# Nine places for split weight chunks, a six-chunk tail per block and a boundary without splits in a float32 two-block transformer

## The chip, the cores and the metric

The kernel runs on one core of a Trainium2 chip. The metric is the time of one execution on the device in microseconds, as the median of several runs. Engines are named as in the profile: PE (TensorE), PEld (its weight loads), DVE (VectorE), ACT (ScalarE), POOL (GpSimd) and SP (SyncE, whose queue issues all DMAs here).

## The reference

Two transformer blocks over 256 tokens of width 1024, batch 1, everything in float32. The norms, the residuals and the feed-forward parts bear on this change:

```python
# first block
x = x + gt1 * _rmsnorm(mix_x, g_post_mix)            # mix_x = concat(pool mixer, attention) @ w_out
y = _sq_relu_mlp(_modulate(x, g_pre_mlp, sh2, sc2), w_mlp_in, w_mlp_out)   # square(relu(h @ w1)) @ w2, width 4096
x = x + gt2 * _rmsnorm(y, g_post_mlp)
# second block
x = x + 0.5 * swiglu(rmsnorm(x, ffn1_norm), ...)     # width 2816
proj = rmsnorm(x, mix_norm) @ w_in
x = x + concat(attention_a, attention_b) @ w_out
x = x + 0.5 * swiglu(rmsnorm(x, ffn2_norm), ...)
x = rmsnorm(x, final_norm)
```

`_modulate(x, g, sh, sc)` is the root-mean-square norm of x times g (1 + sc), plus sh.

## The kernel before

**Chunks and splits.** All weights stream from HBM in the order of `stream_plan` as chunks of 128 x 1024 float32 (512 KB) through seven raw buffers. Float32 accuracy comes from three fast products: ACT rounds a chunk to `hi` (L449), DVE writes the rest `raw - hi` to `lo` (L866), and PE multiplies hi by Th, hi by Tl and lo by Th, where Th and Tl are the activations split in the same way. A split chunk lives in one of `RING = 5` places; ACT may write chunk h only when PE has used chunk h-5 (semaphore `s_used`). `AHEAD = 4` says how far ahead of PE's chunk the splits are put into the programs of ACT and DVE. SP loads a raw buffer again when DVE has written the `lo` of the chunk that was in it.

**Every engine has its own program**, written out by hand in the order in which it runs; waits are on counting semaphores. No scheduler reorders anything.

**Blocks and boundaries.** Four times a product into x is followed by norms and the next product: boundary 0 (w_out, then the MLP), 1 (MLP, then ffn1), 2 (ffn1, then the second mixer's input product), 3 (w_out2, then ffn2). The 256 tokens are two halves i of 128. The last product of a block sums into four PSUM banks, two per half. Its last `TAIL = 4` chunks are the tail: `tail_first`/`out_first` does the four chunks for half 0 and signals `s_part`, then `tail_second`/`second_out` does the same chunks for half 1. Below, "part" is the moment of that signal. In the boundary, for each half: ACT squares the PSUM sums (`gated_squares`, L461), DVE multiplies them by a gain (`gated`, L1086), POOL takes the root (L399), DVE adds to x (`added`, L1103), ACT squares x, DVE sums (L1075), POOL takes the root again, DVE and ACT scale half of x each (`normed`, L1110 and L626). Boundaries 2 and 3 have no first norm: DVE adds PSUM to x at once (L1093). Then PE transposes eight tiles of 128 x 128 (`turned`, L1641) into four banks by turns, so that the fifth waits until the first has been read. ACT writes Th (L634 in boundary 0, where a shift is added, else L637), DVE writes Tl (L1131). In boundary 0 DVE first computes the shifted value itself (L1126) and then subtracts Th (L1117), tile by tile. PE then multiplies the half by the first four chunks of the next block (h0 to h0+3, 24 matmuls of 512 columns; 416 in boundary 2). The second half goes the same way.

The order of ACT and DVE in a boundary (L640 and L1137), where h0 is the next block's first chunk:

```python
split(h0)
e.wait_ge(s_part, b + 1)
gated(b, 0)
added(b, 0)
split(h0 + 1)
normed(b, 0)
e.wait_ge(s_used, h0)
gated(b, 1)
turned(b, 0)
split(h0 + 2)
added(b, 1)
split(h0 + 3)
normed(b, 1)
split(h0 + 4)
turned(b, 1)
```

**The second attention** (L585, L1032, L1577) runs over 32 tiles (16 heads by two halves) in software-pipelined steps n. In each, PE scores a tile and transposes an earlier one, DVE and ACT do the softmax. `fill2(n)` puts other work into chosen steps: PE's whole products with w_out2 chunks 0 to 3 at n = 17, 19, 21, 25, the first-half products of chunks 4, 5, 6 at n = 28, 29, 33, and one split at n = 17, 19, 21, 25 and 28.

**SP's queue** waits at H[26], which is h0+2 of boundary 0, for `s_G` 4 (a gain row that DVE finishes, L978), issues a row load into `gp`, and only then the chunk (L356 to L358, L373).

`big` is a work buffer of 11,776 float32 per partition. It holds q, k, v and other tiles of the two attentions and of the norms around them, and is idle (but for columns 0 to 2047) from the first attention's end to the second mixer.

## Time and profile before

| | us |
|---|---|
| median of 3 runs (lowest, highest) | 928.18 (926.5, 929.54) |
| the profiled execution's own time | 929.46 |
| its span in the profile | 927.5 |
| PE busy | 863.7 |
| DVE busy | 521.0 |
| ACT busy | 444.2 |
| POOL busy | 44.6 |

The time before is the median; the rows come from the profiled execution, which took 929.46 us and of which the profile spans 927.5. Busy time of PE includes the modelled end of pipelined matmuls, so the idle time between its instructions is read from the timeline, which gives it in brackets with the instruction that ended it.

### The profile page before, as it was taken

How to read it: one execution, taken by the hardware profiler on the slowest of the kernel's cores; microseconds unless marked ns; L12 is line 12 of the kernel's file. 1: busy time of each engine (PE TensorE's matmuls, PEld its weight loads, DVE VectorE, ACT ScalarE, POOL GpSimd, SP SyncE). 2: the span in 40 equal slices, each digit the busy share in tenths (PEclk: the TensorE clock that was granted, in tenths of full speed). 3: DMA queues.
4: the chain of work that ended last, by engine and by line, in shares of the span. 5: the costliest groups of instructions: out<-in, count | busy, mean ns of one | idle time of the engine just before them, and what ended most of it. 6: DMA issues, size and time to landing. Idle time of an engine off the chain costs nothing.

```text
span 927.5 us, 13973 instructions
## 1 busy us (share of the span) xinstructions
PE 863.7 (93%) x5434; PEld 734.9 (79%) x5434; DVE 521.0 (56%) x904; ACT 444.2 (48%) x797; POOL 44.6 (5%) x55
## 2 busy tenths in 40 slices
PE   5898899979999999899999999898798899999996
PEld 3696655749999998679999999785465699999995
DVE  2344167476776565665555554677445565555554
ACT  3553045265545444554444444765445554444442
POOL 1000000000000000000000000055100000000000
PEclk9999799979999999999999999998779999999998
DMA  8966338425787565356555554564012265555521
GB/s 325 397 250 248 116 136 319 159 90 163 262 280 226 182 186 172 102 173 231 182 184 182 196 185 146 207 215 158 0 46 69 92 207 179 194 191 181 185 92 46
DMA packets 45105, 165.87 MB, mean 179 GB/s; under 512 B 4976, under 2 KB 5104, under 8 KB 44784
## 3 DMA queue, kind: packets, MB, share of 16 engines
q1 hardware_dynamic: 45040, 164.98, 51.7%
q8 instruction: 44, 0.72, 0.3%
q14 instruction: 21, 0.17, 0.1%
HBM read 163.91 MB, written 1.05 MB: 178 GB/s over the span
## 4 chain that ended last, share of the span: by engine, by line
PE 83%; DVE 5%; ACT 4%; issue 4%; DMA 2%; POOL 1%; SPq 0%; ACTq 0%; DVEq 0%; POOLq 0%
PE ps L1361 13%; PE ps L1363 13%; PE ps L1362 12%; PE ps L1381 12%; PE ps L1383 12%; PE ps L1385 12%; DMA raw<-in_w_mod_p 2%; PE ps L1608 2%; PE ps L1407 1%; ACT hi L449 1%; DVE lo L866 1%; ACT PT L461 1%; PE ps L1795 1%; PE ps L1801 1%; PE ps L1592 1%
## 5 line engine op out<-in xcount | busy, mean ns | idle before, releaser
L866 DVE TENSOR_TENSOR lo<-raw,hi 128x1024 fp32r<-128x1024 f32 (+1 forms) x247 | 298.9, 1218 | 180.2 <-ACT hi L449 180.0
L449 ACT ACTIVATE hi<-raw 128x1024 fp32r<-128x1024 f32 (+1 forms) x247 | 257.1, 1049 | 78.3 <-PE ps L1385 59.9
L1361 PE MATMUL ps<-Th,hi 128*128 128x256 f32 (+1 forms) x960 | 276.1, 288 | 3.1 <-DVE lo L866 1.7
L1363 PE MATMUL ps<-Th,lo 128*128 128x256 f32 (+1 forms) x960 | 275.0, 287 | 0.0
L1362 PE MATMUL ps<-Tl,hi 128*128 128x256 f32 (+1 forms) x960 | 275.0, 287 | 0.0
L1381 PE MATMUL ps<-hi,Th 128*128 128x512 f32 (+2 forms) x524 | 180.6, 404 | 13.9 <-issue 7.0
L1361 PEld LDWEIGHTS ps<-Th,hi 128*128 128x128 f32 x960 | 184.0, 192 | 8.5 <-issue 3.0
L1362 PEld LDWEIGHTS ps<-Tl,hi 128*128 128x128 f32 x960 | 183.9, 192 | 3.7
L1363 PEld LDWEIGHTS ps<-Th,lo 128*128 128x128 f32 x960 | 183.8, 191 | 1.3
L1383 PE MATMUL ps<-lo,Th 128*128 128x512 f32 (+2 forms) x524 | 175.7, 394 | 0.0
L1385 PE MATMUL ps<-hi,Tl 128*128 128x512 f32 (+2 forms) x524 | 175.4, 394 | 0.0
L1381 PEld LDWEIGHTS ps<-hi,Th 128*128 128x128 f32 x524 | 96.0, 193 | 32.7 <-issue 16.4
L1385 PEld LDWEIGHTS ps<-hi,Tl 128*128 128x128 f32 x524 | 100.2, 191 | 21.1
L1383 PEld LDWEIGHTS ps<-lo,Th 128*128 128x128 f32 x524 | 100.4, 192 | 20.5
L679 ACT ACTIVATE Th<-PT 128x256 fp32r<-128x256 f32 x68 | 28.4, 418 | 98.7 <-DVE PT L1211 81.8
L1172 DVE TENSOR_TENSOR Tl<-PT,Th 128x256 fp32r<-128x256 f32 x68 | 29.0, 426 | 32.9 <-ACT Th L679 32.9
L719 ACT ACTIVATE PT<-ps 128x256 f32<-128x256 f32 x40 | 15.4, 385 | 62.9 <-PE ps L1363 62.9
L1407 PE MATMUL ps<-raw,big 128*32 128x256 f32 x320 | 26.4, 447 | 15.0 <-DMA raw<-in_w_mod_p 14.4
L399 POOL TENSOR_TENSOR st<-st 128x1 f32<-128x1 f32 x12 | 6.6, 551 | 583.3 <-DVE st L1075 583.3
L1407 PEld LDWEIGHTS ps<-raw,big 128*32 128x32 f32 x320 | 8.7, 118 | 30.5 <-issue 16.2
L693 ACT ACTIVATE PT<-ps 128x256 f32<-128x256 f32 x28 | 10.7, 383 | 44.5 <-PE ps L1363 44.5
L461 ACT ACTIVATE PT<-x 128x512 f32<-128x512 f32 x24 | 15.0, 629 | 26.4 <-DVE x L1093 10.4
(189 smaller groups left out, 622.4 us busy)
## 6 DMA issues: line engine op xcount, KB each, us to landing
raw<-in_ffn_down SPq DMA_DIRECT2D x44, 512.0 KB, 3.6
raw<-in_w_mod_p SPq DMA_DIRECT2D x40, 512.0 KB, 6.1
raw<-in_ffn_gate SPq DMA_DIRECT2D x40, 512.0 KB, 3.2
raw<-in_ffn_up SPq DMA_DIRECT2D x40, 512.0 KB, 3.2
raw<-in_w_mlp_out SPq DMA_DIRECT2D x32, 512.0 KB, 4.5
raw<-in_w_mlp_in SPq DMA_DIRECT2D x28, 512.0 KB, 4.4
raw<-in_w_out SPq DMA_DIRECT2D x16, 512.0 KB, 5.6
raw<-in_w_in_q SPq DMA_DIRECT2D x8, 512.0 KB, 5.7
```

What stands on the lines that cost most here:

```text
L449: e.activation(hi[h % RING][:, 0:w], raw[n % RAW][:, 0:w], ACT.Copy).then_inc(s_hi, 1)
L461: e.activation(junk[len(squared) % 2][:, 0:512], src, ACT.Square, scale=scale, accum_out=out).then_inc(s, 1)
L679: e.activation(Th[:, f % 8, L:], fbuf[f % 4], ACT.Copy).then_inc(s_ha, 1)
L866: e.tensor_tensor(lo[h % RING][:, 0:w], raw[n % RAW][:, 0:w], hi[h % RING][:, 0:w], ALU.subtract).then_inc(s_lo, 1)
L1172: e.tensor_tensor(Tl[:, f % 8, L:], fbuf[f % 4], Th[:, f % 8, L:], ALU.subtract).then_inc(s_hl, 1)
L1361: e.matmul(o, a, Th[:, k, c0:c1], start=(k == 0), stop=False)
L1362: e.matmul(o, a, Tl[:, k, c0:c1], start=False, stop=False)
L1363: return e.matmul(o, b, Th[:, k, c0:c1], start=False, stop=(k == KT - 1))
L1381: e.matmul(ps[banks[j][n]][:, 0:n_w], lh, a[:, at[n]:at[n] + n_w], start=f, stop=False)
L1383: e.matmul(ps[banks[j][n]][:, 0:n_w], lh, b[:, at[n]:at[n] + n_w], start=False, stop=False)
L1385: m = e.matmul(ps[banks[j][n]][:, 0:n_w], ll, a[:, at[n]:at[n] + n_w], start=False, stop=z)
L1407: m = e.matmul(ps[bank][32 * j:32 * j + 32, c0:c0 + L], w, raw[at % RAW][:, j * L:(j + 1) * L], start=(kh == 0), stop=(kh == 1))
```

## The change

1. **Places.** Eight more pairs of split places are laid over `big`: four are free from w_out chunk 5 to the end of ffn1's block (`EXT1` to `END1`), four others from w_out2 chunk 5 on (`EXT2`). With the ring's five that makes nine. Between `END1` and `EXT2` the ring has five as before. `SLOT[h]` is the place that was written longest ago, `PREV[h]` the chunk that was in it, and `lead(h)` the last chunk that may be split while PE works at h: h+8 with nine places, h+4 with five. All `+ AHEAD` become `lead(...)`, and the splits beside a down product are at most two at a time.
2. **Tail.** `TAIL` goes from 4 to 6, in w_out and w_out2 too, where chunks 2 and 3 are now done for half 0 only before part. The second halves of the first five tail chunks come next, then four transposes, then the sixth, then the other four transposes.
3. **Boundary.** Chunks h0, h0+1 and h0+2 are split before the wait for part, h0+3 after `normed` of half 0, h0+4 at the end. Four tiles are turned before the second half's `gated`, four behind it.
4. **Boundary 0's turn.** ACT writes the shifted even tiles and DVE the odd ones to a small buffer; ACT then copies two tiles at once to Th, and DVE subtracts two at once.

The diff, cut to its core:

```diff
-TAIL = 4
+TAIL = 6
...
+        blocks = [(3072 + 2048 * i, 4096 + 2048 * i) for i in range(4)] + [(8192, 9216), (0, 1024), (2048, 10240),
+                                                                         (3072, 4096)]
+        HI = [u[:, :] for u in hi] + [in_big(f"hi{i + 5}", a)[:, :] for i, (a, _) in enumerate(blocks)]
+        LO = [u[:, :] for u in lo] + [in_big(f"lo{i + 5}", a)[:, :] for i, (_, a) in enumerate(blocks)]
+        SLOT, PREV, newest = [], [], [-1] * len(HI)
+        for h in range(NH):
+            free = list(range(RING)) + list(range(5, 9) if EXT1 <= h < END1 else range(9, 13) if EXT2 <= h else [])
+            slot = min(free, key=lambda n: (newest[n], n))
+            SLOT.append(slot)
+            PREV.append(newest[slot])
+            newest[slot] = h
+
+        def lead(h):
+
+            n = h
+            while n + 1 < NH and PREV[n + 1] < h:
+                n += 1
+            return n
...
-                    if h >= RING:
-                        e.wait_ge(s_used, h - RING + 1)
-                    e.activation(hi[h % RING][:, 0:w], raw[n % RAW][:, 0:w], ACT.Copy).then_inc(s_hi, 1)
+                    if PREV[h] >= 0:
+                        e.wait_ge(s_used, PREV[h] + 1)
+                    if h == EXT2:
+                        e.wait_ge(s_thP, 8)
...
+                    if h == EXT2 + 3:
+                        e.wait_ge(s_pv, 16)
+                    e.activation(HI[SLOT[h]][:, 0:w], raw[n % RAW][:, 0:w], ACT.Copy).then_inc(s_hi, 1)
...
-            def turned(b, i):
+            def turned(b, i, k0, k1):
...
+                    elif k % 2 == 0:
+                        e.wait_ge(s_tp, t_n(b, i, k))
+                        if 8 * i + k >= 4:
+                            e.wait_ge(s_tTl, 8 * i + k - 2)
+                        e.activation(moved(k), src, ACT.Identity, bias=sh2[:, k:k + 1],
+                                     scale=gain[:, k:k + 1]).then_inc(s_tfa, 1)
                     else:
...
+                        e.wait_ge(s_tfa, 4 * i + k // 2 + 1)
+                        e.wait_ge(s_tfd, 4 * i + k // 2 + 1)
+                        e.activation(Th[:, k - 1:k + 1, here], moved_pair(k), ACT.Copy).then_inc(s_tTh, 2)
             def boundary(b):
                 h0 = LASTCH[b] + 1
-                split(h0)
+                split(h0 + 2)
                 e.wait_ge(s_part, b + 1)
                 gated_squares(b, 0)
                 scale_squares(b, 0)
-                split(h0 + 1)
                 normed(b, 0)
+                split(h0 + 3)
+                if b == 0:
+                    e.wait_ge(s_A2, 1)
+                turned(b, 0, 0, 4)
                 e.wait_ge(s_used, h0)
                 gated_squares(b, 1)
-                if b == 0:
-                    e.wait_ge(s_A2, 1)
-                turned(b, 0)
-                split(h0 + 2)
+                turned(b, 0, 4, KT)
                 scale_squares(b, 1)
-                split(h0 + 3)
                 normed(b, 1)
+                turned(b, 1, 0, KT)
                 split(h0 + 4)
-                turned(b, 1)
                 return h0 + 4
...
                 elif what == "down" and f < FM - TAIL:
-                    split(CH["w_mlp_out", f] + AHEAD)
+                    split_by(2, lead(CH["w_mlp_out", f]))
...
-                for at, k in ((17, 0), (19, 1), (21, 2), (25, 3), (28, 4)):
+                for at, k in ((17, 4), (19, 5), (21, 6), (25, 7)):
                     if n == at:
-                        split(CH["w_out2", k] + AHEAD)
+                        split(CH["w_out2", k])
...
-                for k in (1, 2, 3):
-                    out_whole("w_out", k)
+                out_whole("w_out", 1)
+                for k in (2, 3):
+                    out_first("w_out", k)
...
                 first().then_inc(s_part, 1)
-                second()
-                turned(b, 0)
+                second(0)
+                turned(b, 0, 0, 4)
+                second(1)
+                turned(b, 0, 4, KT)
...
-                for at, k in ((17, 0), (19, 1), (21, 2), (25, 3)):
+                for at, k in ((17, 0), (19, 1)):
...
-                for at, k in ((28, 4), (29, 5), (33, 6)):
+                for at, k in ((21, 2), (25, 3), (28, 4), (29, 5), (33, 6)):
```

**How the order moves.** On PE in boundary 0, around the transposes (rows with x2 are the two banks of a tail chunk's second half, rows without are the first product of the MLP). Before:

```order
L1381 MATMUL ps<-hi,Th 128x512 x2
L1383 MATMUL ps<-lo,Th 128x512 x2
L1385 MATMUL ps<-hi,Tl 128x512 x2
L1641 MATMUL ps<-cols,arena 128x128 x8
L1381 MATMUL ps<-hi,Th 128x512
```

With the change (`hi_51` and `lo_59` are places in `big`):

```order
L1423 MATMUL ps<-lo_58,Th 128x512 x2
L1425 MATMUL ps<-hi_50,Tl 128x512 x2
L1682 MATMUL ps<-cols,arena 128x128 x4
L1421 MATMUL ps<-hi_51,Th 128x512 x2
L1423 MATMUL ps<-lo_59,Th 128x512 x2
L1425 MATMUL ps<-hi_51,Tl 128x512 x2
L1682 MATMUL ps<-cols,arena 128x128 x4
L1421 MATMUL ps<-hi_52,Th 128x512
```

One tail chunk's second half now stands between the two groups of four transposes.

On DVE in boundary 0, from the last splits before part to the second `added`. Before:

```order
L866 TENSOR_TENSOR lo<-raw,hi 128x1024 x4
L1086 TENSOR_TENSOR sc<-ps,G 128x512 x2
L1075 TENSOR_SCALAR st<-st 128x1
L1103 SCALAR_TENSOR_TENSOR x<-sc,st,x 128x512 x2
L1075 TENSOR_SCALAR st<-st 128x1
L866 TENSOR_TENSOR lo<-raw,hi 128x1024
L1110 TENSOR_SCALAR arena<-x,st 128x512
L1086 TENSOR_TENSOR sc<-ps,G 128x512 x2
L1075 TENSOR_SCALAR st<-st 128x1
L1126 TENSOR_SCALAR sc<-ps,st 128x128 x2
L1117 TENSOR_TENSOR Tl<-sc,Th 128x128
```

With the change:

```order
L912 TENSOR_TENSOR lo<-raw,hi 128x1024 x2
L1132 TENSOR_TENSOR sc<-ps,G 128x512 x2
L1121 TENSOR_SCALAR st<-st 128x1
L1149 SCALAR_TENSOR_TENSOR x<-sc,st,x 128x512 x2
L1121 TENSOR_SCALAR st<-st 128x1
L1156 TENSOR_SCALAR arena<-x,st 128x512
L912 TENSOR_TENSOR lo<-raw,hi 128x1024
L1170 TENSOR_SCALAR sc<-ps,st 128x128 x2
L1175 TENSOR_TENSOR Tl<-sc,Th 128x2x128 x2
L1132 TENSOR_TENSOR sc<-ps,G 128x512 x2
```

The split has moved from before the scaling (`arena<-x,st`) to behind it, six splits instead of four precede the first gain product (four of them name places in `big` and stand above this piece), and half a turn comes before the second gain product.

On ACT at boundary 3, from the attention's last Th to the scaling. Before:

```order
L602 ACTIVATE Th<-ps 128x256
L461 ACTIVATE PT,st<-x 128x512 x2
L449 ACTIVATE hi<-raw 128x1024
L626 ACTIVATE arena<-x,st 128x512
L637 ACTIVATE Th<-ps,cols 128x128 x8
```

With the change:

```order
L643 ACTIVATE Th<-ps 128x256
L490 ACTIVATE hi_56<-raw 128x1024
L490 ACTIVATE hi<-raw 128x1024 x2
L502 ACTIVATE PT,st<-x 128x512 x2
L667 ACTIVATE arena<-x,st 128x512
```

Three splits now stand between the attention's end and the boundary's first squares; one stood before the scaling.

## Rows read from the trace of the kernel before

**Rows 1.** The page: busy time, share and instructions of each engine.
```profile
PE 863.7 (93%) x5434; PEld 734.9 (79%) x5434; DVE 521.0 (56%) x904; ACT 444.2 (48%) x797; POOL 44.6 (5%) x55
```

**Rows 2.** Windows: stretch, us, busy us PE PEld DVE ACT POOL, clock, DMA share, GB/s.
```profile
181.89:212.39 30.50, 24.00 (x88) 17.58 (x88) 20.91 (x51) 17.42 (x39) 2.20 (x4) 0.83 0.23 77
379.56:405.99 26.43, 21.14 (x88) 16.15 (x88) 16.80 (x35) 15.39 (x39) 2.20 (x4) 0.94 0.29 100
576.57:597.04 20.47, 17.76 (x88) 14.99 (x88) 14.34 (x34) 12.95 (x31) 1.10 (x2) 1.00 0.46 152
721.74:743.90 22.16, 19.65 (x89) 14.98 (x87) 13.46 (x29) 12.59 (x31) 1.11 (x2) 1.00 0.29 96
...
179.17:181.89 2.72, 2.72 (x13) 2.25 (x13) 0.00 (x0) 0.00 (x0) 0.00 (x0) 1.00 1.02 416
```

**Rows 3.** Timeline of PE, boundaries 0 and 1: start us, us, what, [idle before].
```profile
189.07 0.66 PE L1641 MATMUL ps<-cols,arena 128*128 128x128 f32 x4 [1.76 <-DVE arena L1110]
...
191.35 1.74 PE L1641 MATMUL ps<-cols,arena 128*128 128x128 f32 x4 [1.62 <-DVE sc L1126]
...
200.61 0.47 PE L1381 MATMUL ps<-hi,Th 128*128 128x512 f32 x1 [2.50 <-DVE lo L866]
...
386.74 0.66 PE L1641 MATMUL ps<-cols,arena 128*128 128x128 f32 x4 [1.76 <-DVE arena L1110]
...
388.79 1.16 PE L1641 MATMUL ps<-cols,arena 128*128 128x128 f32 x4 [1.40 <-DVE Tl L1131]
...
398.46 0.60 PE L1641 MATMUL ps<-cols,arena 128*128 128x128 f32 x4
...
400.45 0.47 PE L1381 MATMUL ps<-hi,Th 128*128 128x512 f32 x1
```

**Rows 4.** Timeline of DVE, boundary 0.
```profile
181.91 1.41 DVE L1086 TENSOR_TENSOR sc<-ps,G 128x512 f32<-128x512 f32 x2 [3.06 <-PE ps L1385]
...
188.53 0.48 DVE L1110 TENSOR_SCALAR arena<-x,st 128x512 f32<-128x512 f32 x1
...
196.10 1.40 DVE L1103 SCALAR_TENSOR_TENSOR x<-sc,st,x 128x512 f32<-128x512 f32 x2
```

**Rows 5.** Timeline of POOL, boundary 0.
```profile
186.74 0.55 POOL L399 TENSOR_TENSOR st<-st 128x1 f32<-128x1 f32 x1 [2.53 <-DVE st L1075]
...
198.59 0.55 POOL L399 TENSOR_TENSOR st<-st 128x1 f32<-128x1 f32 x1 [7.38 <-DVE st L1075]
```

**Rows 6.** Groups in boundary 0: line, op, shapes, xcount | busy us, mean ns | idle.
```profile
L634 ACT ACTIVATE Th<-ps,st 128x128 fp32r<-128x128 f32 x16 | 6.5, 458 | 2.2 <-PE ps L1641 2.0
L1126 DVE TENSOR_SCALAR sc<-ps,st 128x128 f32<-128x128 f32 x16 | 6.3, 403 | 1.4 <-ACT Th L634 1.4
...
L866 DVE TENSOR_TENSOR lo<-raw,hi 128x1024 fp32r<-128x1024 f32 x4 | 4.9, 1223 | 1.5 <-ACT hi L449 1.5
...
L449 ACT ACTIVATE hi<-raw 128x1024 fp32r<-128x1024 f32 x4 | 4.2, 1042 | 0.0
```

**Rows 7.** The page's part 5: a copy of 128x256 from SBUF.
```profile
L679 ACT ACTIVATE Th<-PT 128x256 fp32r<-128x256 f32 x68 | 28.4, 418 | 98.7 <-DVE PT L1211 81.8
```

**Rows 8.** Timeline of ACT, boundary 3.
```profile
719.15 0.38 ACT L602 ACTIVATE Th<-ps 128x256 fp32r<-128x256 f32 x1 [0.95 <-PE ps L1608]
...
724.77 0.72 ACT L626 ACTIVATE arena<-x,st 128x512 f32<-128x512 f32 x1
```

**Rows 9.** Timeline of DVE, boundary 3.
```profile
721.74 1.29 DVE L1093 SCALAR_TENSOR_TENSOR x<-ps,x 128x512 f32<-128x512 f32 x2 [1.75 <-PE ps L1385]
```

**Rows 10.** Timeline of PE in the second attention.
```profile
697.75 0.30 PE L1592 MATMUL ps<-cols,sc 128*128 128x128 f32 x1 [0.62 <-ACT PT L596]
```

**Rows 11.** Timeline of SP's DMA issue of chunks h0+2 and h0+3, boundary 0.
```profile
171.78 1.15 SPq L373 DMA_DIRECT2D raw<-in_w_mlp_in_rows  x2
```

**Rows 12.** Tile raw, 160 to 200 us: time from issue to landing.
```profile
DMA to landing us min/median/max: 3.5/5.7/7.4
```

**Rows 13.** Windows: a long stretch of the last feed-forward block.
```profile
748.00:900.00 152.00, 152.00 (x1074) 143.17 (x1073) 84.18 (x93) 69.35 (x93) 0.00 (x0) 1.00 0.55 187
```

177 lines of the change are left out of this document (91 added, 86 removed).

## The prediction

> **What bounds the kernel now.** The page comes first: PE is busy 863.7 of 927.5 us, DVE 521 and ACT 444 [rows 1]. In a feed-forward stretch PE is busy for all of 152 us at clock 1.00, while DVE needs 84 us and ACT 69 [rows 13]. There nothing is left to win by splitting further ahead. The windows then show where PE does wait: the four boundaries last 30.50, 26.43, 20.47 and 22.16 us from part to the end of the eight products ahead, 99.6 us together [rows 2]. The work in one is known. Two chunks' second halves take 2.72 us, so one takes 1.36 [rows 2]. A boundary holds four of them (5.4), eight products of the same 512 columns at six matmuls a chunk over both halves, which is 24 matmuls or 5.45 a half (4.4 in boundary 2, 416 columns), and 16 transposes, for which I put 2.0. That makes 18.3 us, 16.2 in boundary 2, 71.1 in all. So 28 us are waits and slow clock, and that is the ceiling of the gain.
>
> The timeline of PE names them [rows 3]. In boundary 0 PE waits 1.76 us for the scaled x (L1110), 1.62 for turned tiles, and 2.50 for a `lo` (L866). In boundary 1 it waits 1.76 and 1.40 before the first products. [...]
>
> **Part by part.** I count from part, t = 0, and chunk halves move with it: the two tail chunks that are added put 2.72 us of PE work behind part that stood before it. So a boundary gains what it took before, plus 2.72, minus what it takes now, wherever PE was full before part. It was ahead of boundary 0 (clock 1.00, PE busy 2.72 of 2.72 [rows 2]), and I take the same of 1 and 2.
>
> *The chain of half 0.* In boundary 0 gains start on DVE at 181.91 [rows 4] and POOL's second root ends at 187.29 [rows 5], 5.4 later. DVE scaled x only at 188.53 [rows 4], since a split of 1.22 us [rows 6] stood in between. Now it is scaled at 5.4 + 0.48 = 5.9. PE does five second halves until 6.8, so the wait of 1.76 goes in both boundaries, with 0.9 us to spare. The sixth half (6.8 plus four transposes to 8.7) covers the first turn.
>
> *Boundary 0.* After scaling, ACT splits h0+3 (its scaling 0.72 and the split 1.04 us [rows 6, 8] put the end at 7.2) and DVE follows to 8.4. The turn by pairs has no row. Its upper bound is the old one: a tile cost ACT 0.46 and DVE 0.40 [rows 6], plus the subtraction. Its lower bound is a pair copy alone at 0.42 [rows 7]. I take 0.46 + 0.42 a pair on ACT, and 0.40 + 0.40 + 0.42 on DVE, since each pass is nearest to those rows. Four tiles are then finished at 10.4; PE starts on products at 9.9 and has two chunks until 12.6. DVE's second gains (1.41 [rows 4]) end at 11.8, ACT turns the other tiles until 13.6, DVE until 14.2. PE waits 0.8 and ends half 0 at 16.1. From `added` to the root was 196.10 to 199.14, 3.0 us [rows 4, 5]: 17.3, scaled at 17.7, so PE waits 1.6. From the first transpose to the first product takes 2.0 (398.46 to 400.45 [rows 3]): 19.7, and 5.4 more is 25.1.
> Two things are added. Chunk h0+2 must now be split before part is even waited for. It is issued at 171.78 [rows 11], behind SP's wait for the gain row, and lands a median 5.7 us later [rows 12]. With 1.04 and 1.22 [rows 6] its `lo` is there at 179.8, while part moves to 181.89 - 2.72 = 179.2. That is 0.7 late, and DVE starts its gains that much later. And the waits of 1.6 and about 1.3 around the second transposes look like those of boundary 1, so I take one fall of the clock, 1.4. Boundary 0: 27.2, against 30.5 + 2.7 = 33.2. **Gain 6.0.**
>
> *Boundary 1.* ACT and DVE turn as before, four tiles each time. DVE is finished with the first four at 9.5, PE starts at 9.7 and does all four chunks until 15.15 without a wait. The second gains end at 10.9, the other four tiles at 12.4, x is scaled at 15.9. PE waits 0.8, then 2.0 and 5.4: 23.4. I take no fall of the clock. 26.4 + 2.7 - 23.4: **gain 5.75.**
>
> *Boundary 2* has one root only. Scaled x comes long before 6.8; products run from 9.2 to 13.6, x of half 1 is scaled by 12.9; 2.0 and 4.4 more make 20.0. 20.5 + 2.7 - 20.0: **gain 3.2.**
>
> *Boundary 3.* The attention's last Th ends at 719.53 [rows 8]. Three splits now follow on ACT, and DVE's three end at 719.53 + 1.04 + 3 x 1.22 = 724.2, while it began to add at 721.74 [rows 9]: 2.5 late. From there to the scaling was 3.0 (724.77 [rows 8]), so x is scaled at 6.0, before 6.8; the delay is hidden, by 0.8. Products start at 9.7, end at 15.15, then 2.0 and 5.45: 22.6 against 22.2. The work that moved in comes from the attention, where PE isn't full: behind the product at n = 21 it already waits 0.62 for ACT [rows 10]. What the attention gives back for 2.72 us is between 0 and 2.7; I take 1.1, nearer to nothing because of that wait, with one split less in it. **Gain 0.7.**
>
> *Nothing* is booked for the deeper places in long stretches (PE full there, [rows 13]) and for the last block's six-chunk tail: after the last product the norm of half 1 runs as before. If the splits did not fit beside PE, that cover would be gone (third rival).
>
> The sum is 6.0 + 5.75 + 3.2 + 0.7 = 15.6 us. Against the profiled execution (929.46) it gives 913.8; that one lies 1.3 above the median, and against the median of 928.2 it is **912.6 us**.
>
> **Rivals.** *The clock keeps falling.* Boundary 1 fell after waits of 1.76 and 1.40 with four transposes between [rows 3], and 2 and 3 did not. If it falls in 1 as well (1.4), and in the attention, where three half products of 1.36 would take 4.1 more, with its 1.1 not given back, the gain is 15.6 - 6.6 = 9.0: 919. For it: the attention's PE work gets thinner. Against: the waits get shorter in total. [...]
>
> *All cover works.* No fall of the clock in boundary 0 (1.4 back), chunk h0+2 in time (0.7) and the attention gives back all 2.7 (1.6 more): 19.3, so 909; with half of the second transposes' waits hidden too, 907.
>
> *The debt is paid behind the boundary* (slower). After each boundary ACT and DVE must split four chunks more to be eight ahead, two at each place, ahead of the activations on the same engine that PE waits for. Four `lo` are 4.9 us of DVE [rows 6], four times 19.6 us. If PE waited for all of it, the result would be 4.0 slower, 932; it decides from 15.6 us on. Against it: DVE is idle 68 of 152 us there [rows 13], and the hidden tiles have a lag of two to five steps.
>
> *The change doesn't do what it says*: the second halves wait as the first did. If only the waits of half 0 go (1.76 twice, 1.62, 1.40), the gain is 6.5: 922.
>
> **Chances.** Forecast 0.62, all cover 0.12, clock 0.12, only half 0 0.05, no change 0.05, slower 0.04. A measurement can tell 0.3% (2.8 us) from no change: faster 0.91, same 0.05, slower 0.04. The bounds of the attention (0 to 2.7), of the clock (0 to 5) and of the turn reach from 907 to 919; the range of eight in ten is 905.5 to 919.5, which takes in both nearer rivals.
>
> **What would show it.** PE without a wait of over 0.5 us before the first transposes of all boundaries; part of boundary 0 near 179.2, DVE's gains a little behind; waits of 1.6 and 0.8 before the transposes of half 1 in boundaries 0 and 1; granted clock 0.9 or more in boundary 0 and 1.00 in 1; about 27, 23, 20 and 22.5 us per boundary. A PE wait for `lo` or Tl inside the feed-forward blocks, or a boundary 1 over 26 us, would make the forecast wrong.

## The result and the profile after

The changed kernel takes **912.23 us** (median of 4 runs, 911.67 to 913.14) where the kernel before takes 927.51 beside it (926.5 to 929.54): a ratio of 0.9837, 95% interval 0.9823 to 0.9851. The forecast was 912.6. The profiled execution took 913.14 with a span of 911.2; the one before had 929.46 and 927.5.

The page, part 1, against [rows 1]:

```profile
PE 859.1 (94%) x5434; PEld 732.0 (80%) x5434; DVE 515.2 (57%) x888; ACT 440.3 (48%) x797; POOL 44.5 (5%) x55
```

PE is busy 4.6 us less, though it does the same work, and the span is 16.3 us shorter. The windows of the four boundaries, from part to the end of the products ahead, answer to [rows 2] (stretch, us, busy us of PE, PEld, DVE, ACT and POOL, clock, DMA share, GB/s):

```profile
179.31:206.63 27.32, 23.84 (x100) 18.19 (x100) 16.41 (x34) 15.47 (x37) 2.19 (x4) 0.94 0.33 124
371.00:394.26 23.26, 22.23 (x100) 17.23 (x100) 14.35 (x33) 13.58 (x37) 2.20 (x4) 1.00 0.13 43
561.13:581.37 20.24, 19.63 (x100) 17.28 (x100) 12.39 (x32) 11.27 (x29) 1.10 (x2) 1.00 0.11 33
705.27:727.74 22.47, 21.86 (x101) 17.29 (x100) 13.12 (x30) 11.39 (x30) 1.12 (x2) 1.00 0.36 117
```

With the two halves that moved in (2.72 us for the two), boundary 0 went from 33.2 to 27.3, boundary 1 from 29.2 to 23.3, boundary 2 from 23.2 to 20.2 and boundary 3 from 24.9 to 22.5. PE's timeline of boundary 0, the rows with a wait, against [rows 3] (start, us, what, [idle before <- who ended it]):

```profile
189.14 0.44 PE L1682 MATMUL ps<-cols,arena 128*128 128x128 f32 x2 [0.55 <-ACT sc L680]
...
193.12 0.50 PE L1421 MATMUL ps<-hi,Th 128*128 128x512 f32 x1 [0.75 <-DVE Tl L1175]
...
197.45 0.66 PE L1682 MATMUL ps<-cols,arena 128*128 128x128 f32 x4 [1.31 <-DVE arena L1156]
...
198.42 0.41 PE L1682 MATMUL ps<-cols,arena 128*128 128x128 f32 x2 [0.31 <-ACT sc L680]
...
199.27 0.33 PE L1682 MATMUL ps<-cols,arena 128*128 128x128 f32 x1 [0.44 <-ACT sc L680]
```

There is no wait before the first transposes any more (1.76 before), none of 2.50 for a `lo`, and one of 1.31 for the scaled x of half 1. Boundary 1 had 1.76 and 1.40 [rows 3], 1.52 for a `lo` and 0.61; boundary 2 had 1.29 before its fifth transpose, 0.18 and 0.63 for a `lo`, and 0.61. From the kernel before:

```profile
397.00 0.47 PE L1381 MATMUL ps<-hi,Th 128*128 128x512 f32 x1 [1.52 <-DVE lo L866]
...
583.74 1.02 PE L1641 MATMUL ps<-cols,arena 128*128 128x128 f32 x4 [1.29 <-DVE Tl L1131]
...
587.21 0.43 PE L1381 MATMUL ps<-hi,Th 128*128 128x416 f32 x1 [0.18 <-DVE lo L866]
...
589.22 0.42 PE L1381 MATMUL ps<-hi,Th 128*128 128x416 f32 x1 [0.63 <-DVE lo L866]
```

Of these, boundary 2 keeps the 0.61, and boundary 1 has two left:

```profile
386.67 0.66 PE L1682 MATMUL ps<-cols,arena 128*128 128x128 f32 x4 [0.41 <-DVE arena L1156]
...
387.94 0.49 PE L1682 MATMUL ps<-cols,arena 128*128 128x128 f32 x2 [0.61 <-DVE Tl L1164]
```

The start of boundary 0 on ACT and DVE. The split of chunk h0+2 comes ahead of part, and waits for its transfer:

```profile
177.33 1.06 ACT L490 ACTIVATE hi<-raw 128x1024 fp32r<-128x1024 f32 x1 [4.22 <-DMA raw<-in_w_mlp_in_rows]
...
178.42 1.23 DVE L912 TENSOR_TENSOR lo<-raw,hi 128x1024 fp32r<-128x1024 f32 x1 [1.32 <-ACT hi L490]
...
179.56 0.69 DVE L1132 TENSOR_TENSOR sc<-ps,G 128x512 f32<-128x512 f32 x1
```

Part is at 179.31 and gains start at 179.56. In the attention, the two chunks at n = 21 and 25 are now multiplied for half 0 only. PE waits longer there, 1.26 us each time where it was 0.62 [rows 10]:

```profile
681.83 0.30 PE L1633 MATMUL ps<-cols,sc 128*128 128x128 f32 x1 [1.26 <-ACT PT L637]
...
688.81 0.30 PE L1633 MATMUL ps<-cols,sc 128*128 128x128 f32 x1 [1.26 <-DVE PT L1089]
```

For the account, the program is cut at the ends of the boundaries. With the stretch that leads to it, boundary 0 gained 5.8 us, boundary 1 6.0, boundary 2 3.9, and boundary 3 with the attention 0.5; the last stretch gained 0.1. That makes the 16.3.

### The profile page after: what moved, and what is told of

Same layout as the page of the kernel before. It is cut to its first block, busy times and chain, and to the rows that moved or that the text cites. A ratio compares the mean times of both kernels' runs of the same rounds, so it can differ in the third digit from the quotient of the medians.

```text
span 911.2 us, 13975 instructions
## 1 busy us (share of the span) xinstructions
PE 859.1 (94%) x5434; PEld 732.0 (80%) x5434; DVE 515.2 (57%) x888; ACT 440.3 (48%) x797; POOL 44.5 (5%) x55
## 4 chain that ended last, share of the span: by engine, by line
PE 72%; DVE 2%; POOL 1%; ACT 1%; issue 1%; DVEq 0%; ACTq 0%; POOLq 0%
PE ps L1401 11%; PE ps L1402 11%; PE ps L1403 11%; PE ps L1421 11%; PE ps L1423 11%; PE ps L1425 11%; PE ps L1649 2%; PE ps L1839 1%; PE ps L1633 1%; PE ps L1845 1%; PE ps L1682 1%; PE ps L1841 1%; POOL st L456 0%; ACT PT L502 0%; POOL st L462 0%
## 5 line engine op out<-in xcount | busy, mean ns | idle before, releaser
L490 ACT ACTIVATE hi<-raw 128x1024 fp32r<-128x1024 f32 (+1 forms) x247 | 253.8, 1047 | 65.0 <-PE ps L1425 41.5
L1401 PE MATMUL ps<-Th,hi 128*128 128x256 f32 (+1 forms) x960 | 276.2, 288 | 3.1 <-DVE lo L912 1.7
L1401 PEld LDWEIGHTS ps<-Th,hi 128*128 128x128 f32 x960 | 183.8, 191 | 8.6 <-issue 3.0
L1421 PE MATMUL ps<-hi,Th 128*128 128x512 f32 (+2 forms) x524 | 179.9, 402 | 9.5 <-issue 7.3
L1403 PEld LDWEIGHTS ps<-Th,lo 128*128 128x128 f32 x960 | 183.5, 191 | 1.3
L1421 PEld LDWEIGHTS ps<-hi,Th 128*128 128x128 f32 x524 | 94.9, 191 | 27.1 <-issue 9.1
L765 ACT ACTIVATE PT<-ps 128x256 f32<-128x256 f32 x40 | 15.3, 383 | 55.4 <-PE ps L1403 55.4
L647 ACT ACTIVATE sc<-sc,st 128x128 f32<-128x128 f32 (+1 forms) x32 | 14.5, 455 | 27.0 <-DVE st L1106 26.8
```

Source lines behind the costliest of these rows:

```text
L490: e.activation(HI[SLOT[h]][:, 0:w], raw[n % RAW][:, 0:w], ACT.Copy).then_inc(s_hi, 1)
L1401: e.matmul(o, a, Th[:, k, c0:c1], start=(k == 0), stop=False)
L1403: return e.matmul(o, b, Th[:, k, c0:c1], start=False, stop=(k == KT - 1))
L1421: e.matmul(ps[banks[j][n]][:, 0:n_w], lh, a[:, at[n]:at[n] + n_w], start=f, stop=False)
```

## The experiments

Twelve kernels, all made from the changed one. In the table, each profile is one execution, and **two stretches that no experiment touches vary by themselves**. The opening up to part of boundary 0 took 176.9 to 181.1 us in the kernels that have six halves there, with a granted clock of 0.94 to 0.97; in the two with four it took 185.0 and 179.5. The stretch from the end of boundary 2 to the end of boundary 3, the attention in it, took 143.9 to 149.6. And boundary 0 came mostly with a clock of 0.94 or 1.00. So a part is judged by its own boundary at equal clock, and the medians only by their intervals. Boundaries 0, 1 and 2 run from part to the end of their products; the fifth column is the stretch with the attention and boundary 3. Boundary 1 had a clock of 0.94 in the kernel before and 1.00 in all others; boundary 2 had 1.00 in all.

| kernel | b0 us (clock) | b1 | b2 | attention + b3 | median us | ratio to before (95%) |
|---|---|---|---|---|---|---|
| before | 30.50 (0.83) | 26.43 | 20.47 | 146.86 | 927.5 | 1 |
| changed | 27.32 (0.94) | 23.26 | 20.24 | 146.37 | 912.23 | 0.984 (0.982 to 0.985) |
| tail4 | 25.47 (1.00) | 22.00 | 17.41 | 147.56 | 917.43 | 0.988 (0.983 to 0.992) |
| chain_splits | 30.42 (0.89) | 26.85 | 21.94 | 145.53 | 921.29 | 0.994 (0.991 to 0.997) |
| places_only | 31.56 (0.84) | 22.01 | 17.40 | 143.91 | 918.58 | 0.991 (0.989 to 0.994) |
| lead4 | 25.54 (1.00) | 23.24 | 20.20 | 146.28 | 907.42 | 0.976 (0.972 to 0.981) |
| turn_after | 26.12 (0.93) | 24.42 | 22.06 | 148.00 | 915.48 | 0.987 (0.982 to 0.992) |
| b0_after | 27.25 (0.94) | 23.24 | 20.19 | 146.35 | 911.84 | 0.983 (0.980 to 0.987) |
| old_turn | 27.82 (0.94) | 23.25 | 20.22 | 145.18 | 913.82 | 0.984 (0.979 to 0.989) |
| lo_late | 27.03 (0.94) | 24.19 | 20.21 | 146.29 | 911.30 | 0.982 (0.978 to 0.986) |
| big_even | 25.87 (1.00) | 23.24 | 20.02 | 143.89 | 910.95 | 0.982 (0.978 to 0.986) |
| ring_behind_cols | 27.23 (0.94) | 23.35 | 20.23 | 147.42 | 909.82 | 0.980 (0.974 to 0.985) |
| ring_kind | 25.57 (1.00) | 23.31 | 20.19 | 145.77 | 910.25 | 0.982 (0.979 to 0.985) |
| combined | 25.60 (1.00) | 23.37 | 20.25 | 149.55 | 909.85 | 0.982 (0.979 to 0.985) |

tail4 and places_only have two halves fewer behind part; 2.72 us is added to their boundaries 0 to 2 before they are compared with the changed kernel, and nothing when they are compared with the one before. A loss between two medians is a difference of kernels that ran at different times, each beside its own runs of the kernel before, whose medians were 927.0 to 929.5.

### tail4: four halves instead of six

```diff
-TAIL = 6
+TAIL = 4
-                out_whole("w_out", 1)
-                for k in (2, 3):
-                    out_first("w_out", k)
+                for k in (1, 2, 3):
+                    out_whole("w_out", k)
...
-                for at, k in ((17, 0), (19, 1)):
+                for at, k in ((17, 0), (19, 1), (21, 2), (25, 3)):
```

> The changed kernel with four split second halves in a block's tail in place of six: the output projection's chunks 2 and 3 run whole again, everything else as changed. Theory (the two further halves stand as cover at the boundary, 2.72 us the pair): about +6.6 us against the changed kernel's 912.2, so 918.8: +2.7 in boundary 0, +2.7 in boundary 1, where the products still wait without them, +0.4 in boundary 2 and +0.8 in boundary 3, where there was next to no wait to cover. Rival 1 (taking the splits out of the norms' chain did it all): within 1 us of the changed kernel. Rival 2 (the tail's halves did it all): 923 or more.

Measured: +5.2 us in the median. Boundary 0, at clock 1.00, is 28.2 against lead4's 25.5 at the same clock: **+2.65, as expected**. Boundary 1 is 24.7, +1.5 only, and boundary 2 is 20.1, no loss at all. Its stretch with boundary 3 is 1.2 longer. PE waits again before the first transposes, 1.78 us in boundary 1:

```profile
383.55 0.66 PE L1681 MATMUL ps<-cols,arena 128*128 128x128 f32 x4 [1.78 <-DVE arena L1156]
...
392.00 0.66 PE L1681 MATMUL ps<-cols,arena 128*128 128x128 f32 x4 [0.51 <-DVE arena L1156]
```

Cover pays, but in boundaries 1 and 2 less than two chunk halves. In boundary 1 the first transposes start 5.98 us behind part here (377.57 to 383.55), since the scaled x comes no sooner. Three halves cover 4.1 of that and five cover 6.8, which is more than it needs. In boundary 2, with one root, PE does not wait there with three halves either. I had expected 6.6 us in all and 2.7 in boundary 1.

### chain_splits: six halves, the splits back inside the chain

```diff
-                split(h0 + 2)
+                split(h0)
                 e.wait_ge(s_part, b + 1)
                 gated_squares(b, 0)
                 scale_squares(b, 0)
+                split(h0 + 1)
                 normed(b, 0)
-                split(h0 + 3)
...
                 turned(b, 0, 4, KT)
+                split(h0 + 2)
                 scale_squares(b, 1)
+                split(h0 + 3)
```

(the same on DVE)

> The changed kernel with the splits of chunks h0+1 to h0+3 back inside the norms' chain, at the four points of the kernel before, on ScalarE and VectorE; six second halves and the nine places stay. Theory: each split inside the chain lengthens it, and with six halves the chain sets the end in boundaries 0 and 1: +2.6 us each there, about +1.2 in boundary 2 and +0.5 in boundary 3, in all +5.5 (+4 to +9), so 917 to 921. Rival (the six halves cover the splits as well): 0 to +1 us.

Measured: **+9.1 us in the median**, at the end of my range of 4 to 9. Boundary 1 is 3.6 longer at the same clock, boundary 2 1.7, boundary 0 3.1 with a clock of 0.89 against 0.94. The rival is out. PE's waits in boundaries 0 and 1:

```profile
187.37 0.66 PE L1686 MATMUL ps<-cols,arena 128*128 128x128 f32 x4 [0.28 <-DVE arena L1158]
...
195.85 0.47 PE L1425 MATMUL ps<-hi,Th 128*128 128x512 f32 x1 [3.23 <-DVE lo L914]
...
200.14 0.77 PE L1425 MATMUL ps<-hi,Th 128*128 128x512 f32 x1 [2.36 <-DVE lo L914]
```

```profile
388.60 0.47 PE L1425 MATMUL ps<-hi,Th 128*128 128x512 f32 x1 [1.64 <-DVE lo L914]
...
392.89 0.47 PE L1425 MATMUL ps<-hi,Th 128*128 128x512 f32 x1 [2.68 <-DVE lo L914]
...
395.55 0.75 PE L1686 MATMUL ps<-cols,arena 128*128 128x128 f32 x3 [0.61 <-DVE Tl L1166]
```

The first transposes wait 0.28 us or nothing: there the six halves do cover the chain. The loss is at another place than I had expected. PE is at the products of half 0 and waits for the `lo` of the third and fourth chunk, 3.23 and 2.36 us in boundary 0, 1.64 and 2.68 in boundary 1. So it is not enough that a split is outside the norm; it must be done before its product's turn.

### places_only: nine places, deeper splitting and the turn in two groups

tail4, chain_splits and old_turn (below) together: TAIL 4, the four old split points, boundary 0's turn by tiles. Two things stay of the new order. The turn of half 0 is in two groups of four, on PE around the last second half and on ACT and DVE around the second half's gains; and h0+4 is split behind the turns. So the expectation's "everything at the boundaries as before the change" isn't what the kernel does, and what it shows is the places **with** the turn in two groups.

> The changed kernel with everything at the boundaries as before the change (four second halves, the splits of chunks h0 to h0+3 at their old points inside the chain, boundary 0's turn tile by tile), so that of the change only the nine places and the deeper splitting in the long stretches are left. Theory (the places buy nothing by themselves): each boundary as long as before, PE idle in the stretch before each boundary's end as before (6.5, 5.3, 2.7 and 3.9 us); only chunks in the large buffer run faster as the weight-load operand, which the first feed-forward block shows as 1 us; total 926 at the clock of the profile shown before the change (924 to 928). Rival (splits that can run ahead relieve the boundaries in any order): 922 or less.

Measured: 918.58, a ratio of 0.991 (0.989 to 0.994). **My theory fell**: boundaries 1 and 2 are not as long as before, and the median is 8.6 us below that of the kernel before (3.0 of what its profile shows lies in the stretch with the attention, which varies by itself). Boundary 1 takes 22.01 in place of 26.43, and boundary 2 17.40 in place of 20.47. Two causes are mixed in this. One is in DVE's splits in boundary 1. Before there were four, at 385.06, 391.34, 395.63 and 397.26. Here there is one, the split of h0+4 behind the turns:

```profile
371.01 1.23 DVE L907 TENSOR_TENSOR lo<-raw,hi 128x1024 fp32r<-128x1024 f32 x1 [0.40 <-ACT hi L490]
...
396.32 1.23 DVE L907 TENSOR_TENSOR lo<-raw,hi 128x1024 fp32r<-128x1024 f32 x1 [0.59 <-ACT hi L490]
```

A split call goes up to a chunk number and does nothing if that chunk is already split. With nine places the splitting in the long stretch runs so far ahead that h0 to h0+3 are done by 372.2, before part at 378.18, and the four old points inside the chain are empty. The boundary with the old order then waits like tail4's, because it is tail4's (22.01 and 22.00, 17.40 and 17.41). Boundary 0 has no such stretch in front of it (the places open with w_out's chunk 5), and there it takes 31.56 us, 1.1 more than before the change. The old waits for splits are still in it:

```profile
186.66 1.12 PE L1676 MATMUL ps<-cols,arena 128*128 128x128 f32 x4 [3.00 <-DVE arena L1151]
...
195.66 0.47 PE L1416 MATMUL ps<-hi,Th 128*128 128x512 f32 x1 [1.02 <-DVE lo L907]
...
199.94 0.76 PE L1416 MATMUL ps<-hi,Th 128*128 128x512 f32 x1 [2.66 <-DVE lo L907]
```

It also shows what six halves cost: with TAIL 6 the splitting beside the down products ends two chunks sooner (f < FM - TAIL), and three chunks are left for the boundary in chain_splits (387.23, 391.52 and 398.01 on DVE, with h0+4). The two ways overlap: the places take the splits out of boundaries 1 and 2, or the new order takes them out. The new order alone does it in boundary 0.

The other cause is the turn in two groups. The waits of 1.40 (boundary 1) and 1.29 us (boundary 2) before the fifth transpose are gone in places_only, and turn_after, further down, has them back at 1.80 and 1.29 with the places kept. What is left for the places are the waits for a `lo`, 1.52 in boundary 1 and 0.18 and 0.63 in boundary 2, and in boundary 1 the way from part to the first transposes, 5.95 us (378.18 to 384.13) where it was 7.18 (379.56 to 386.74), a split shorter. The places with the old turn were not run, so how the 4.4 and 3.1 us divide is not shown. By turn_after, with six halves, the turn is worth 1.2 and 1.8 of them. In boundary 1 the clock rose from 0.94 to 1.00 as well. A fall cost 1.78 us where it was measured, in boundary 0 between the changed kernel and lead4.

### lead4: never more than four chunks ahead

```diff
-            return n
+            return min(n, h + RING - 1)
```

> The changed kernel with the nine places kept but the splitting in the long stretches never more than four chunks ahead, as before the change. Theory (PE waits for nothing in those stretches, so depth buys nothing): within 1 us of the changed kernel's 912.2, and each stretch between two boundaries within 0.3 us. Rival (the deeper places carry part of the gain, by covering waits after a boundary): 914 or more, with PE waits for lo behind the boundaries.

Measured: 907.42, a ratio of 0.976 (0.972 to 0.981), and boundaries 1 and 2 at 23.24 and 20.20, as in the changed kernel. With six halves and the new order the depth buys nothing; the rival is out. The median is even 4 us lower, and its interval does not touch that of the changed kernel. Of the 4.2 us between the profiles, 1.83 lie in the opening, where each engine runs the same instructions in the same order, 1.78 in boundary 0 with its clock at 1.00:

```profile
177.48:203.02 25.54, 22.15 (x101) 17.00 (x99) 16.28 (x34) 15.54 (x37) 2.19 (x4) 1.00 0.28 111
366.87:390.11 23.24, 22.23 (x101) 17.22 (x100) 14.34 (x33) 13.57 (x37) 2.19 (x4) 1.00 0.31 113
557.00:577.20 20.20, 19.59 (x100) 17.27 (x99) 12.38 (x32) 11.25 (x29) 1.10 (x2) 1.00 0.30 107
```

and 0.54 in a gap of PE in the MLP that is 0.86 us long where it is 1.40 in the changed kernel. Up to the end of boundary 0 the depth changes no order, so 3.6 of the 4.2 us have another cause, most likely how the clock fell (0.97 against 0.95 in the opening); that isn't shown for the medians. That shallower is really faster isn't excluded.

### turn_after and b0_after: where the first turn stands

```diff
-                turned(b, 0, 0, 4)
                 e.wait_ge(s_used, h0)
                 gated_squares(b, 1)
-                turned(b, 0, 4, KT)
+                turned(b, 0, 0, KT)
```

(the same on DVE and PE; in b0_after for boundary 0 alone)

> The changed kernel with the turns of the next block's half 0 behind all six second halves instead of four of them ahead of the last half. Theory: the last half no longer covers the eviction and splitting of four turned tiles. In boundaries 0 and 1 the turn was about as late as its place, so it costs 0.5 us each; in boundaries 2 and 3, where nothing else is waited for, about 1.1 each: +3 us (2 to 4.5), so 915.2. Rival (the wait is for the chain ahead of the turn, and the place of the turn is free): 0 to +0.7 us.

Measured: 915.48, +3.2 us, as expected, with other shares. Boundary 1 is 1.2 longer, boundary 2 1.8, the stretch with boundary 3 1.6. The wait that comes is the one that the interleaving hides, before the fifth transpose:

```profile
379.08 1.01 PE L1680 MATMUL ps<-cols,arena 128*128 128x128 f32 x4 [1.80 <-DVE Tl L1163]
...
569.85 1.02 PE L1680 MATMUL ps<-cols,arena 128*128 128x128 f32 x4 [1.29 <-DVE Tl L1163]
```

I had 0.5 in boundary 1 and 1.1 in boundary 2. Boundary 0 went the other way, 1.2 shorter at a clock of 0.93, so it was tried alone.

> The changed kernel with boundary 0 alone turning half 0 behind all six second halves, on all engines; boundaries 1 to 3 as changed. When all four turned late, boundary 0's waits of PE fell from 3.36 to 2.81 us and the other three lost 1.2, 1.3 and 1.3. Theory (in boundary 0 the gains of half 1 come first on VectorE, so the waits of 0.75 and 1.31 us ahead of the third chunk's products and of the second transposes go, and one of about 1.5 us ahead of the fifth transpose comes): PE's waits in boundary 0 2.8, the boundary 0.6 us shorter at equal clock, the others at 23.2, 20.2 and 20.3. Rival (that boundary was shorter by its clock alone): no gain, 0 to +0.5.

Measured: boundary 0 at 27.25 against 27.32, the others unchanged, 911.84. **No gain: the rival holds.** PE waits 1.62, 0.55, 0.82, 0.31 and 0.44 us, 3.7 in all against 3.4. The 1.2 us of one execution didn't come back in another with the same order in this boundary.

### old_turn: boundary 0's turn by tiles

```diff
-                    elif k % 2 == 0:
+                    else:
...
-                        e.activation(Th[:, k - 1:k + 1, here], moved_pair(k), ACT.Copy).then_inc(s_tTh, 2)
+                        e.activation(Th[:, k, here], src, ACT.Identity, bias=sh2[:, k:k + 1],
+                                     scale=gain[:, k:k + 1]).then_inc(s_tTh, 1)
```

(and DVE shifts all tiles itself, as before the change)

> The changed kernel with boundary 0's turn tile by tile as before, in place of pairs shared by ScalarE and VectorE. Theory: the pairs save a little between the transposes and the first products of each half, and only there: boundary 0 longer by 0.8 us (0 to 1.5) at the same clock, the other three unchanged. Rival (one of the two engines, not the form, sets the turn): boundary 0 within 0.2 us.

Measured: boundary 0 at 27.82 against 27.32 at clock 0.94, the others the same to 0.02. The pairs are worth **0.5 us** in this execution; I had expected 0.8. PE's waits in the boundary sum to 3.4 us in both, so I can't name a single wait that they save.

### lo_late: DVE's last split behind the additions

```diff
                 normed(b, 0)
-                split(h0 + 3)
+                if b > 1:
+                    split(h0 + 3)
...
                 added(b, 1)
+                if b < 2:
+                    split(h0 + 3)
```

> The changed kernel with VectorE's lo split of chunk h0+3 in boundaries 0 and 1 moved from ahead of the first turn to behind the two additions to x of half 1. Theory (VectorE's 1.23 us there delays the first turn, the gains of half 1 and so the second transposes): the wait of 1.31 us ahead of boundary 0's second transposes falls to 0.6, boundary 0 shorter by 0.7 and boundary 1 by 0.5 at equal clock, total -1.2 us. Rival (the chunk is then late for the products of half 0): the wait turns up in the fourth chunk's products of half 0, and the boundary stays within 0.2 us.

Measured: boundary 1 is 0.93 **longer**, boundary 0 0.3 shorter. The rival names the right wait, but put it at 0.2 us at most. In boundary 0 the 1.31 ahead of the second transposes is gone, and PE now waits more for this `lo` in the products of half 0:

```profile
193.80 0.47 PE L1424 MATMUL ps<-hi,Th 128*128 128x512 f32 x1 [2.74 <-DVE lo L912]
```

```profile
383.51 0.47 PE L1424 MATMUL ps<-hi,Th 128*128 128x512 f32 x1 [1.95 <-DVE lo L912]
```

In boundary 1 the place that the change gives to h0+3, between scaling and turn, is the better of the two; in boundary 0 they differ by 0.3 us.

### big_even, ring_behind_cols, ring_kind: where a chunk lies

In the changed kernel PE's pace depends on the place of the chunk. From its timeline in the first feed-forward block (L1421 starts a chunk as the moving operand, L1401 the first and the eighth of a chunk's eight triples as the weight-load operand). The chunks at 417.26 and 420.01 lie in the ring, those at 422.88 and 425.69 in `big`:

```profile
417.26 0.63 PE L1421 MATMUL ps<-hi,Th 128*128 128x512 f32 x2
...
420.01 0.28 PE L1401 MATMUL ps<-Th,hi 128*128 128x256 f32 x1
...
422.52 0.28 PE L1401 MATMUL ps<-Th,hi 128*128 128x256 f32 x1
...
422.88 0.28 PE L1401 MATMUL ps<-Th,hi 128*128 128x256 f32 x1
...
425.33 0.28 PE L1401 MATMUL ps<-Th,hi 128*128 128x256 f32 x1
...
425.69 0.63 PE L1421 MATMUL ps<-hi,Th 128*128 128x512 f32 x2
...
428.49 0.28 PE L1401 MATMUL ps<-Th,hi 128*128 128x256 f32 x1
```

Moving operand: 2.75 us in the ring, 2.80 in `big`. Weight load, first to eighth: 2.51 in the ring, 2.45 in `big`. In the whole program, of the 44 chunks in `big` that go through the weight load 43 take 2.45 or 2.46 us. Of the 72 in the ring 63 take 2.51 or 2.52, the others more. In the kernel before, where all 116 lie in the ring, none takes less than 2.51.

big_even moves `cols` behind `big`; ring_behind_cols moves the ring behind `cols`:

```diff
-        cols = sb("cols", [P, NCOLS])
         ...
         big = sb("big", [P, 11776])
+        cols = sb("cols", [P, NCOLS])
```

Offsets are worked out here from the widths of the tiles in kernel.py, and count from the ring's start: no run shows the addresses themselves. `cols` has 1461 columns, 5,844 bytes, which is 724 past a multiple of 1024; the 736 of ring_kind's expectation is this rounded up to a multiple of 32. Every other tile between the ring and `big` has a multiple of 1024 bytes. So `big` is offset by `cols` in the changed kernel and has no offset in big_even; in ring_behind_cols the ring takes the place modulo 1024 that `big` keeps.

> [...] In the changed kernel a chunk that lies in the large buffer has 24 first-half matmuls in 2.80 us where a chunk in the ring takes 2.87 to 2.88 (as the weight-load operand), and 2.80 against 2.75 as the moving operand. Theory A (alignment of the operand): both differences go, 2.88 and 2.75 everywhere, total +0.5 to +2 us. Theory B (the region of the memory, not the alignment): the differences stay and the total is within 0.5 us.

> [...] Theory A (the offset sets the pace, wherever the tile lies): all weight-load chunks, ring and large buffer, at 2.45 us in place of 2.51 for the ring; chunks as the moving operand 2.80 in place of 2.75; between the boundaries the first feed-forward block 1.5 us shorter or more. Theory B (the region sets it): ring chunks stay at 2.51.

Measured: both differences follow the place that the order of allocation gives, and not the region. In big_even the chunk in `big` goes from 2.45 to 2.52, like the ring's:

```profile
419.15 0.28 PE L1401 MATMUL ps<-Th,hi 128*128 128x256 f32 x1
...
421.66 0.28 PE L1401 MATMUL ps<-Th,hi 128*128 128x256 f32 x1
...
422.02 0.28 PE L1401 MATMUL ps<-Th,hi 128*128 128x256 f32 x1
...
424.54 0.28 PE L1401 MATMUL ps<-Th,hi 128*128 128x256 f32 x1
```

In ring_behind_cols the ring's chunk goes from 2.51 to 2.45, and the moving one from 2.75 to 2.80:

```profile
416.87 0.63 PE L1421 MATMUL ps<-hi,Th 128*128 128x512 f32 x2
...
419.67 0.28 PE L1401 MATMUL ps<-Th,hi 128*128 128x256 f32 x1
...
422.12 0.28 PE L1401 MATMUL ps<-Th,hi 128*128 128x256 f32 x1
```

Between the boundaries the first feed-forward block is 1.0 us longer in big_even (167.9 against 166.9) and 1.0 shorter in ring_behind_cols (165.9); the last stretch is 1.7 shorter there (181.8 against 183.5). I had expected 1.5 for the first feed-forward block. The total of big_even was expected 0.5 to 2 us longer and came out 1.3 shorter, with boundary 0 at a clock of 1.00 and 2.5 less in the stretch with the attention, so the median doesn't show the 1.0.

ring_kind tries 32 bytes alone, in three of the ring's places: a chunk that goes through the weight load is to lie 32 past a multiple of 64 bytes there, counted as above, and a chunk that is the moving operand at a multiple of 64.

```diff
+        ring = [sb(f"{n}{i}", [P, W + 8 * (i < 3)], F32R) for i in range(RING) for n in ("hi", "lo")]
+            o = 8 if (tiles is HI) == (plan[H[h]][0] in STAT) else 0
+            return (hi if tiles is HI else lo)[s][:, o:o + W]
```

> [...] Theory (a 32-byte offset is enough): weight-load chunks of places 0 to 2 at 2.45 us in place of 2.51, those of 3 and 4 at 2.51, moving chunks of the ring as before (2.75 for the whole chunk); about 45 chunks of 0.07, -3 us at equal clock. Rival (a coarser offset counts: the large buffer lies 736 bytes past the ring's own position modulo 1024): all ring places stay at 2.51, total unchanged.

Measured: weight-load chunks at 2.46, 2.50 and 2.45 us in places 0, 1 and 2, and 2.51 in places 3 and 4, where nothing was changed. Places 0 and 2 came as expected and place 1 didn't, though all three are offset alike, 32 bytes past a multiple of 64 counted from the ring's start. The moving chunks there, at multiples of 64, take 2.79 and not 2.75. So "32 past 64" is **not the rule**. The wider ring also moved Th and Tl by 192 bytes, so the distance to the other operand changed too; whether that counts stays open. The median is 910.25; I had expected 3 us less than the changed kernel's, and it is 2.0 less.

### combined

ring_behind_cols, and SP's wait for the gain row ahead of H[34] in place of H[26].

> The changed kernel with the ring behind the small column table, so that every split chunk goes through the weight load at the faster pace, and with SP's wait for the gain row moved from ahead of stream chunk 26 to ahead of chunk 34, so that chunk h0+2 of boundary 0 is issued earlier. Theory: with all weight-load chunks at 2.45 us the stretches are 0.3 us (MLP), 1.0 (first feed-forward) and 1.7 (second) shorter than in the changed kernel, as in the run with the ring moved alone; VectorE starts its gains in boundary 0 with part and not 0.25 us behind it; in all -3.2 us at equal clock, a median of 909. Rival 1 (the pace of the moving operand, 2.80 for 2.75, and the clock of the opening take it back): 911 to 913. Rival 2 on the gain row (the chunk's landing is not set by SP's wait): the 0.25 us stays.

Measured: 909.85 (905.92 to 915.84), a ratio of 0.982 (0.979 to 0.985). The three long stretches are 0.4, 1.0 and 1.7 shorter, as expected, and gains start with part:

```profile
179.55 1.41 DVE L1132 TENSOR_TENSOR sc<-ps,G 128x512 f32<-128x512 f32 x2 [1.24 <-PE ps L1425]
```

The 0.25 us are gone; rival 2 is out. But its stretch with the attention took 149.55 us, 3.2 more, at a clock of 0.87:

```profile
578.65:728.20 149.55, 135.06 (x572) 98.17 (x570) 85.96 (x257) 80.39 (x196) 31.61 (x31) 0.87 0.31 110
```

so most of the gain isn't in the total. The changed kernel has 0.91 there. I had expected 909, and the interval overlaps that of the changed kernel. No version here is shown to beat it but lead4, and that with the doubt above. ring_behind_cols had 147.42 in this stretch, also above 146.37; whether a shifted layout costs something in the attention, or the clock just fell so, wasn't separated.

## Why the prediction was right

**The sum.** Forecast 6.0 + 5.75 + 3.2 + 0.7 = 15.6 us; measured 5.8, 6.0, 3.9 and 0.5, and 0.1 at the end, 16.3 in all. PE's waits in the four boundaries, counted from 0.15 us, fell from 16.8 to 5.6 us, which is the mechanism that was forecast. That the median is off by 0.4 us only is in part luck: 1.0 us came from the pace of chunks in `big`, which the sum doesn't have, and the fall of the clock in boundary 0, which it has, is there in this profile and missing in five others.

**Boundary 0**, 27.2 forecast, 27.32 measured. The wait of 1.76 is gone, as the chain's 5.9 us against 6.8 of halves said. Of the waits, 0.8 became 0.75 and 1.6 became 1.31. Chunk h0+2 was late by 0.25 and not 0.7: ACT waited 4.22 us for its transfer, but its `lo` was there at 179.6, not 179.8, and part came at 179.31. The turn by pairs, which had no row, came as estimated: DVE finished the four tiles of the first group 10.6 us behind its start (10.4 forecast) and those of the second at 14.4 (14.2). Not in my working was the 0.55 us before the seventh transpose, where ACT's share of the pair turn is behind. One fall of the clock was put at 1.4. No row and no run shows this term, nor the 5 us that the range allows for the clock: both were estimates of mine. In the trace of before, matmuls of 512 columns start every 0.43 us in this boundary where the granted clock is 0.50 (193.74 and 194.17), and every 0.23 where it is 1.00 (195.66 and 195.89). What a fall costs, changed and lead4 show: they have the same waits in this boundary, at 0.94 and at 1.00, and differ by **1.78**. The errors (0.4 too little for the clock, 0.45 too much for the late chunk, and the smaller ones above) nearly cancel.

**Boundary 1**, 23.4 forecast, 23.26 measured, at clock 1.00. The wait before the second transposes is 0.41, not 0.8; a second one, 0.61, lies inside the 2.0 that I put for transposes and turn.

**Boundary 2**, 20.0 forecast, 20.24 measured, a gain of 2.95 where I had 3.2. The other 1.0 of its 3.9 lies in the stretch ahead of it, and is the pace of chunks in `big`, which I did not know: the same stretch is 1.0 longer in big_even. "Nothing is booked for the deeper places in long stretches" was right for waiting: PE's idle time before the weight-load matmuls is 3.1 us in the whole program, as before the change. It was wrong for the pace.

```profile
L1361 PE MATMUL ps<-Th,hi 128*128 128x256 f32 (+1 forms) x960 | 276.1, 288 | 3.1 <-DVE lo L866 1.7
L1401 PE MATMUL ps<-Th,hi 128*128 128x256 f32 (+1 forms) x960 | 276.2, 288 | 3.1 <-DVE lo L912 1.7
```

(the kernel before, then the changed one; busy us, mean ns, idle before)

**Boundary 3**, 22.6 forecast, 22.47 measured. DVE's additions start at 707.46, 2.2 us behind part (2.5 forecast), x is scaled 5.7 behind it (6.0), and PE's first transposes don't wait. From the end of boundary 2 to part the time fell from 124.70 to 123.90, so the attention gave back 0.8 of 2.7; I had 1.1. The two waits grew by 1.3 together, which fits the 1.9 it kept. But this stretch took 121.5 to 126.9 us in kernels that have the same program there, so the 0.8 of one pair of profiles confirms nothing.

**The rivals.** The clock stayed at 1.00 in boundary 1, and was 0.89 before and after the change from boundary 2 to part of boundary 3, so the first is out. In turn_after eight transposes stood in one group in boundary 1 with a wait of 1.80 us among them, and the clock was 1.00 all the same. No run shows what makes the clock fall. The 4.1 us for three half products at a fallen clock is an estimate; by the starts 0.43 and 0.23 us apart above, 18 matmuls would take about 3.6 more. *All cover works* came in one part: boundary 0 at 1.00 in five of the twelve kernels, though not in the changed one. No debt was paid behind a boundary (the row above), and the second halves did what they say.

**What I had wrong is the shares, not the sum.** By the working, halves and splits each buy their own part and the places nothing. The boundaries of the runs side by side, with 2.72 us added where four halves stand behind part, and the clock where it isn't 1.00:

| | before | places_only | tail4 | chain_splits | turn_after | changed |
|---|---|---|---|---|---|---|
| places and depth | no | yes | yes | yes | yes | yes |
| turn in two groups | no | yes | yes | yes | no | yes |
| new order, pairs | no | no | yes | pairs | yes | yes |
| six halves | no | no | no | yes | yes | yes |
| boundary 0 | 33.2 (0.83) | 34.3 (0.84) | 28.2 | 30.4 (0.89) | 26.1 (0.93) | 27.3 (0.94) |
| boundary 1 | 29.2 (0.94) | 24.7 | 24.7 | 26.9 | 24.4 | 23.3 |
| boundary 2 | 23.2 | 20.1 | 20.1 | 21.9 | 22.1 | 20.2 |

In boundary 0 the places and the turn in two groups buy nothing, the order most (6.1, the clock in it), and the halves 2.65 more at equal clock. That is as forecast. In boundary 1 the places and the turn together buy 4.4, the order nothing on top, and the halves 1.5 more if the order goes with them; without it they lose 2.1, since they cut the run-ahead short. In boundary 2 the places and the turn together buy all of it, and there the turn alone is worth 1.8 with six halves.

So the prediction has two terms in the wrong place. It books the places at nothing. That holds for the sum, since lead4 has the same boundaries without the depth; but where the order is old, the depth takes the splits out of boundaries 1 and 2, as DVE's rows of places_only show. And "the chain of half 0" says that the splits leave the chain because they are written elsewhere. They leave it because they are done before part, and there were two ways to that, of which lead4 and places_only each show one. The turn in two groups, which has no price of its own in the sum, carries 1.2 us in boundary 1 and 1.8 in boundary 2.

## What to carry to other kernels

A split call that does nothing if the chunk is already split makes the run-ahead part of the order: count where the splits really fall before pricing the point where they are written. Cover behind a dependency and work moved out of it are not two gains to be added: the six halves taken away cost 5.2 us, the new split points 9.1, and both with the pairs 6.4. Take each away with the other in place. And judge a part by its own stretch at equal clock, since stretches that were not touched moved by 4 to 5 us from one execution to the next. An experiment named "only" should be compared with the kernel before line by line: here it had kept the turn in two groups.
